# Running two gate panels ahead of the norm's root in a hybrid attention trunk

## The reference

```
h = h + mlp_sq_relu(rmsnorm(h, norm_mlp[i]), w_up[i], w_down[i])
gate = jax.nn.sigmoid(rmsnorm(h, norm_ple[i]) @ w_ple_gate[i])
h = h + gate * (p[i] @ w_ple_proj[i])
```

## Time and profile before

| | us |
|---|---|
| median of three runs | 2636.97 |
| lowest, highest | 2633.31, 2637.98 |
| profiled execution | 2633.67 |
| its span, from first to last instruction | 2632.1 |
| PE busy | 2530.4 (96%) |
| DVE busy | 1895.3 (72%) |
| ACT busy | 1144.4 (43%) |
| POOL busy | 792.5 (30%) |

### The profile page before, as it was taken

One profiled execution on the slowest core, in us unless ns is written; L12 is line 12 of the kernel. 1 busy time (PEld: TensorE's weight loads), 2 busy tenths in 40 slices (PEclk: granted clock), 3 DMA queues, 4 the chain that ended last, 5 costly groups with the idle time before them and its releaser, 6 DMA issues. The chain is left out here.

```text
span 2632.1 us, 32491 instructions
## 1 busy us (share of the span) xinstructions
PE 2530.4 (96%) x11896; PEld 2080.5 (79%) x11896; DVE 1895.3 (72%) x2562; ACT 1144.4 (43%) x1862; POOL 792.5 (30%) x586
## 2 busy tenths in 40 slices
PE   7999999899999999999999999999999998999998
PEld 6878888687888778887778888878788886888777
DVE  7677655657666789998765667566766668999876
ACT  6555433534444444444442324254444444444353
POOL 2000000023332456666420000002323336666642
PEclk9999999999999999999999999999999999999999
DMA  3000000122323432332221011112233233323112
GB/s 131 31 27 25 29 28 25 46 83 87 118 101 118 134 113 100 115 110 68 77 96 41 25 33 32 32 41 88 92 105 119 101 130 111 128 97 120 65 56 81
DMA packets 78641, 207.64 MB, mean 79 GB/s; under 512 B 8673, under 2 KB 10737, under 8 KB 78497
## 3 DMA queue, kind: packets, MB, share of 16 engines
q1 hardware_dynamic: 75552, 195.85, 21.9%
q0 software_dynamic: 2224, 7.54, 0.8%
q10 hardware_dynamic: 720, 2.36, 0.2%
HBM read 163.25 MB, written 42.47 MB: 78 GB/s over the span
## 5 line engine op out<-in xcount | busy, mean ns | idle before, releaser
L738 PE MATMUL gemm_ps<-a_hi,whi 128*128 128x512 f32 x1024 | 424.8, 415 | 19.2 <-DVE a_lo L1917 10.7
L740 PE MATMUL gemm_ps<-a_hi,wlo 128*128 128x512 f32 x1024 | 403.3, 394 | 0.0
L739 PE MATMUL gemm_ps<-a_lo,whi 128*128 128x512 f32 x1024 | 402.2, 393 | 0.0
L738 PEld LDWEIGHTS gemm_ps<-a_hi,whi 128*128 128x128 f32 x1024 | 194.4, 190 | 59.9 <-issue 20.2
L740 PEld LDWEIGHTS gemm_ps<-a_hi,wlo 128*128 128x128 f32 x1024 | 193.7, 189 | 43.0
L1245 POOL TENSOR_TENSOR hid_raw<-hid_raw 128x512 f32<-128x512 f32 x120 | 197.3, 1653 | 97.3 <-DVE a_blocks L2393 34.6
L739 PEld LDWEIGHTS gemm_ps<-a_lo,whi 128*128 128x128 f32 x1024 | 194.7, 190 | 32.8 <-issue 1.4
L2306 DVE TENSOR_TENSOR wlo<-wraw,whi 128x512 fp32r<-128x512 f32 (+1 forms) x204 | 181.0, 888 | 32.5 <-ACT whi L1601 31.9
L2306 DVE TENSOR_TENSOR wlo<-wraw_a,whi 128x512 fp32r<-128x512 f32 (+1 forms) x204 | 180.0, 883 | 33.8 <-ACT whi L1601 32.8
L1601 ACT ACTIVATE whi<-wraw_a 128x512 fp32r<-128x512 f32 (+1 forms) x204 | 122.6, 602 | 174.7 <-PE s_ps L740 134.1
L738 PE MATMUL s_ps<-b_blocks_hi,whi 128*128 128x512 f32 x448 | 178.9, 399 | 13.2 <-DVE wlo L2306 9.2
(11 more groups left out here) (390 smaller groups left out, 6376.4 us busy)
## 6 DMA issues: line engine op xcount, KB each, us to landing
wraw<-panels SPq DMA_DIRECT2D x90, 512.0 KB, 3.5
wraw<-folds SPq DMA_DIRECT2D x60, 512.0 KB, 4.3
wraw_a<-folds SPq DMA_DIRECT2D x60, 512.0 KB, 4.2
hid_raw<-hidden SPq DMA_DIRECT2D x120, 256.0 KB, 3.7
hidden<-sumsq SPq DMA_DIRECT2D x64, 256.0 KB, 3.9
hidden<-zs SPq DMA_DIRECT2D x32, 256.0 KB, 2.1
hidden<-zt SPq DMA_DIRECT2D x32, 256.0 KB, 2.0
h<-x_t SPq DMA_DIRECT2D x11, 512.0 KB, 5.3
```

Source lines behind the costliest of these rows:

```text
L738: nc.tensor.matmul(out, hi_w, hi_x, start=start, stop=False, skip_group_check=True)
L739: nc.tensor.matmul(out, hi_w, lo_x, start=False, stop=False, skip_group_check=True)
L740: return nc.tensor.matmul(out, lo_w, hi_x, start=False, stop=stop, skip_group_check=True)
```

## The change

- **PE.** Gate panel 1 is numbered before projection panel 3 and runs before the norm sums. The weight stream is put in the same order.
- **Raw units.** DVE copies the four units of gate panels 0 and 1 unscaled to SBUF (`keep_raw`, into `gate_raw`, two tiles of a_hi that lie free) and multiplies them with rstd once the root is there (`scale_raw`). ACT's sigmoid of these waits on the new semaphore `raw_scaled`.
- **ACT.** All high parts of tiles 2 to 7 come before the first square.
- **p.** The high and low part of p's first half move from block 4 to block 3 of the last turn, the low part of the first projection panel from block 4 to block 5. POOL's `tail_adds(2)` waits for that low part of p.
- **Last pair.** The four additions in SBUF leave `down_out` and come after the low part of the second projection panel (`last_adds`). Two of them change places, and the counts of `next_hi` with them.
- **DVE.** The order of copies and splits behind it is changed.

```diff
--- before.py
+++ after.py
@@ -182,7 +182,7 @@
...
     s["tail"] = s["wo"] + KT
-    s["ple"] = [s["tail"] + j for j in (0, 1, 2, 4)]
+    s["ple"] = [s["tail"] + j for j in (0, 1, 2, 5)]
     s["gate"] = s["tail"] + 3
@@ -328,6 +328,8 @@
...
+
+        gate_raw = m["p_skip"][:, 3:5].rearrange("p o (h n) -> p o h n", h=2)
         hid_raw, a_blocks = m["hid_raw"], m["a_blocks"]
@@ -442,6 +444,7 @@
...
         p_hi_ready, p_lo_ready = sem("p_hi_ready"), sem("p_lo_ready")
+        raw_scaled = sem("raw_scaled")
         sig_ready, h_ready, o_gated = sem("sig_ready"), sem("h_ready"), sem("o_gated")
@@ -1035,6 +1038,7 @@
...
                                 unit(Idx(st["gate"]), half, b_hi, b_lo, Idx(st["x_ple"]), places=places)
+                        panel(Idx(st["gate"] + 1), b_hi, b_lo)
                         norm_sums(st["norm"] + 2, to_ps)
@@ -1052,7 +1056,6 @@
...
                         last.then_inc(unit_ready, 1)
-                panel(Idx(st["tail"] + 5), b_hi, b_lo)
                 stage(Idx(st["tail"] + 6), KT - 2 - (LATE if layer else 0), b_hi, b_lo)
@@ -1306,7 +1309,7 @@
...
                 last_sums()
-                gp.wait_ge(blk_lo_ready, BLOCKS * turn_of(layer, TURNS))
+                gp.wait_ge(p_lo_ready, 2 * layer + 1)
                 tail_adds(2)
@@ -1669,7 +1672,7 @@
...
                     else:
-                        act.wait_ge(tail_last, 4 * layer + {(0, 1): 3, (1, 0): 4, (1, 1): 2}[o % 2, half])
+                        act.wait_ge(tail_last, 4 * layer + {(0, 1): 2, (1, 0): 3, (1, 1): 4}[o % 2, half])
                     A(b_hi[:, o, half_cols(half)], piece(o, half), ACT.Copy,
@@ -1735,27 +1738,35 @@
...
                             w_hi(Idx(st["tail"]))
+                        if n == LAST and j == 3:
                             act.wait_ge(p_loaded, 16 * (layer + 1))
...
                 A(p_hi[1], p_raw[:, :, half_cols(1)], ACT.Copy).then_inc(p_hi_ready, 1)
-                for o in range(6):
+                for o in range(2, 4):
                     for half in range(2):
-                        next_hi(o + 2, half)
-                        tail_square(o, half)
-                    if o in (1, 3):
-                        w_hi(Idx(st["tail"] + 2 + o // 2))
-                w_hi(Idx(st["tail"] + 4))
-                for o in (6, 7):
+                        next_hi(o, half)
+                w_hi(Idx(st["tail"] + 2))
+                for o in range(4, KT):
+                    for half in range(2):
+                        next_hi(o, half)
+                w_hi(Idx(st["tail"] + 3))
+                for o in range(KT):
                     for half in range(2):
                         tail_square(o, half)
+                    if o == 2:
+                        w_hi(Idx(st["tail"] + 4))
                 w_hi(Idx(st["tail"] + 5))
+                w_hi(Idx(st["tail"] + 6))
                 norm_root_of(st["norm"] + 2, to_ps)
                 def sigmoid(p, o, half):
-                    act.wait_ge(unit_free, p.times(2).at(half + 1))
+                    if p is None:
+                        act.wait_ge(raw_scaled, 4 * layer + o.times(2).at(half + 1))
+                    else:
+                        act.wait_ge(unit_free, p.times(2).at(half + 1))
                     act.wait_ge(sq_added, (o.times(2) + (16 * (st["norm"] + 3) + half)).at(-1))
@@ -1763,21 +1774,21 @@
...
-                def gate(o, weights=True):
+                def gate(o, weights=True, raw=False):
                     p = o + (st["tail"] + 4)
                     for half in range(2):
-                        sigmoid(p, o, half)
+                        sigmoid(None if raw else p, o, half)
                         finish_gated(o, half)
...
                 for half in range(2):
-                    sigmoid(Idx(st["gate"]), Idx(0), half)
-                w_hi(Idx(st["tail"] + 6))
+                    sigmoid(None, Idx(0), half)
+                w_hi(Idx(st["tail"] + 7))
                 for half in range(2):
                     finish_gated(Idx(0), half)
+                gate(Idx(1), False, True)
                 if layer == 0:
-                    gate(Idx(1))
                     with act.Fori(1, KT // 2 - 1) as i:
@@ -1786,10 +1797,9 @@
...
                 else:
-                    for o in range(1, KT - LATE):
-                        gate(Idx(o), o == 1)
-                        if o > 1:
-                            late_w_hi(o - 2)
+                    for o in range(2, KT - LATE):
+                        gate(Idx(o), False)
+                        late_w_hi(o - 2)
@@ -2359,9 +2369,6 @@
...
                         V.tensor_tensor(p7, b["E"], p7, ALU.add).then_inc(fold_read, 1)
-                        if n == LAST:
-                            dve.wait_ge(fold_read, read + 5)
-                            V.tensor_tensor(p7, p7, u2, ALU.add).then_inc(tail_last, 1)
                     if j == 3:
@@ -2371,15 +2378,17 @@
...
                         V.tensor_tensor(out, b["A" if j == 2 else "E" if j == 6 else "D"], out, ALU.add).then_inc(fold_read, 1)
-                    if n == LAST and j in (5, 6):
-                        if j == 5:
-                            dve.wait_ge(tail_last, 4 * layer + 1)
-                            V.tensor_tensor(piece(2 * q + 1, 1), piece(2 * q + 1, 1), p7, ALU.add).then_inc(tail_last, 1)
-                            dve.wait_ge(fold_read, read + 6)
-                            V.tensor_tensor(piece(2 * q, 1), piece(2 * q, 1), u2, ALU.add).then_inc(tail_last, 1)
-                        else:
-                            dve.wait_ge(fold_read, read + 7)
-                            V.tensor_tensor(piece(2 * q + 1, 0), piece(2 * q + 1, 0), p7, ALU.add).then_inc(tail_last, 1)
+
+                def last_adds():
+
+                    q, read = PAIRS - 1, reads(layer, LAST)
+                    u2, p7 = SUM_U2[q], SUM_P7[q]
+                    dve.wait_ge(fold_read, read + 7)
+                    V.tensor_tensor(p7, p7, u2, ALU.add).then_inc(tail_last, 1)
+                    V.tensor_tensor(piece(2 * q, 1), piece(2 * q, 1), u2, ALU.add).then_inc(tail_last, 1)
+                    dve.wait_ge(tail_last, 4 * layer + 1)
+                    V.tensor_tensor(piece(2 * q + 1, 0), piece(2 * q + 1, 0), p7, ALU.add).then_inc(tail_last, 1)
+                    V.tensor_tensor(piece(2 * q + 1, 1), piece(2 * q + 1, 1), p7, ALU.add).then_inc(tail_last, 1)
@@ -2462,11 +2471,13 @@
...
                             split_of(EARLY_TILES[n, j], 1)
-                        if n == LAST and j == 4:
+                        if n == LAST and j == 5:
                             w_lo(Idx(st["tail"]))
+                        if n == LAST and j == 3:
                             p_low(0)
...
                 w_lo(Idx(st["tail"] + 1))
+                last_adds()
                 n = st["norm"] + 3
@@ -2497,45 +2508,60 @@
...
+                def keep_raw(o, half):
+                    dve.wait_ge(unit_ready, 2 * (st["gate"] + o) + half + 1)
+                    V.tensor_copy(gate_raw[:, o, half], bank(half)).then_inc(unit_free, 1)
+
+                def scale_raw(o, half):
+                    V.tensor_tensor(zt[:, half], gate_raw[:, o, half], rstd[:, half_cols(half)],
+                                    ALU.mult).then_inc(raw_scaled, 1)
+
...
                 w_lo(Idx(st["tail"] + 2))
+                split_of(2, 0)
                 pp_out(1, 0)
-                split_of(2, 0)
                 split_of(2, 1)
+                split_of(3, 0)
                 pp_out(1, 1)
                 w_lo(Idx(st["tail"] + 3))
-                split_of(3, 0)
+                split_of(3, 1)
                 pp_out(2, 0)
-                split_of(3, 1)
-                split_of(4, 0)
-                split_of(4, 1)
+                for half in range(2):
+                    split_of(4, half)
                 pp_out(2, 1)
-                for o in (5, 6):
+                for o in (5, 6, 7):
                     for half in range(2):
...
                 w_lo(Idx(st["tail"] + 4))
-                for half in range(2):
-                    split_of(7, half)
-                w_lo(Idx(st["tail"] + 5))
+                for o in range(2):
+                    for half in range(2):
+                        keep_raw(o, half)
+                    w_lo(Idx(st["tail"] + 5 + o))
                 norm_scale(n - 1)
                 for half in range(2):
-                    gate_in(Idx(st["gate"]), half)
+                    scale_raw(0, half)
                 for e in range(2):
                     pp_out(3, e)
-                w_lo(Idx(st["tail"] + 6))
+                w_lo(Idx(st["tail"] + 7))
                 for half in range(2):
...
                         next_lo(Idx(0), 0)
+                for half in range(2):
+                    dve.wait_ge(h_ready, 16 * layer + half + 1)
+                    scale_raw(1, half)
+                    if half == 0:
+                        next_lo(Idx(0), 1)
```

(13 more changed lines are left out.)

## The result

The changed kernel takes 2639.41 us (median, 2636.63 to 2643.59) where the kernel before, run beside it, takes 2635.83 (2631.94 to 2639.16). The ratio is 1.0015, with 95% between 1.0009 and 1.0021: 4.0 us slower, 2.4 to 5.5 (the two medians differ by 3.6). That is small, 0.15%, but clear of no change, and of the other sign than the 2.7 us gained that I forecast. The profiled execution has a span of 2635.0 us, before 2632.1.

What follows compares the result with a forecast made beforehand. It took PE, busy 96% of the span, to bound the kernel. Gains of 1.3 us in layer 0 and 1.4 in layer 1 summed to 2.7, giving 2634.3 us on the median's scale, range 2625 to 2641.5.

Steps and rivals of the forecast that it cites:

- the term for the wait behind the root: New PE waiting for DVE's reading of panel 2's bank after the root: 2.0 us in layer 0, 0.5 in layer 1.
- The gap itself: PE's stop before gate panel 3, where DVE reads panel 2's bank late: 2.0 us in layer 0, 0.5 in layer 1.
- the 13.0 us: Behind the root, DVE does tile 0 as before until 13.0 us behind the sums; gate panel 1's work follows.
- Ahead of the root: Stretch up to gate panel 2, claimed to start 3.3 us earlier in layer 0 and 1.9 in layer 1.
- the gap before the fold's last block product: PE's 2.75 us wait for the fold's last product, claimed to vanish with the early low part of p.
- the gap at the second projection panel: New PE wait of 1.7 us for the first copy, behind the last pair's additions moved later.
- panel 0: Gate panel 0: PE gaps of 1.35 us at its start, 2.9 for split (5,0), 1.3 and 0.3 for tile 7.
- the last: PE's wait before gate panel 1 for the weights' low part and the first raw copy: 1.8 us.
- Less contention: Rival: POOL slows DVE's splits less ahead of gate panel 1; 2623 us at half contention, 2619 at none; 16 in 100.
- The clock falls in the new gaps: Rival: falls in gate panels 1 and 3, 2.3 us each; 2638.9 us with one per layer, 2643.5 with two; 12 in 100.
- It does nothing: Rival: the wait after the root, longer by the sigmoid's place behind the square, takes back 3.3 us; 2637 us; 12 in 100.
- The rule weighed: DVE splits beside POOL: exclusion for whole instructions would give about 1.96 us; the prediction took the trace's 1.75.

Runs made afterwards that it cites:

- whi_early: Changed kernel with ACT making the next weights' high part before finishing the gate's second half; 0.9999 of the kernel before.
- before_whi_early: Kernel before, with ACT making the next weights' high part before it finishes the gate's second half; 0.9989 of the kernel before, 2.9 us faster.
- in_place: Changed kernel, scaling raw panel 1 in its own buffer and reading panel 2's first half before finishing panel 1; 1.0014 of the kernel before.
- no_raw: Kernel before with every part of the change but the raw units, gate panel 1 staying behind the sums; 1.0021 of the kernel before, 5.5 us slower.
- raw_only: Changed kernel with only PE's order and the raw units left of the change; 1.0041 of the kernel before, 10.8 us slower.
- both_late: Changed kernel with the edits of in_place and whi_early, POOL's squares starting only when tile 4 is split; 0.9963 of the kernel before, 0.9965 in its repeat.
- both: Changed kernel with the edits of in_place and whi_early together; 0.9984 of the kernel before.
- short_sums: Changed kernel with POOL copying one column in place of fourteen of the sixteen additions of squares in each layer; 0.9978 of the kernel before.

## Why the prediction was wrong

**The step that failed** is the term for the wait behind the root, 2.0 and 0.5 us, and in it the last sentence on the scaling: "PE's next panels take 10.9 us each against DVE's 7 to 8, so this is paid once." The 7 to 8 us are DVE's busy time. Its period is 11.32 us in layer 0's loop, because each turn passes several times between DVE and ACT, and that is longer than PE's 10.9. A late start was therefore not caught up there, but grew. The term of 2.0 us in layer 0 measured 7.25: 2.88 for the gap, then 1.8 for the start of panel 4 (12.67 us behind panel 3), 1.3 for three panels at 11.32, 1.0 more for the last norm sum, and 0.3 in pauses of 0.15 us and less. The term of 0.5 in layer 1 measured 2.68: 1.39, then 1.0 more in front of the late panels, and small ones. whi_early and before_whi_early show how much of it is the chain: with the wait for ACT out of it DVE is back to waiting for PE, and the cost is 4.8 and 1.6 us. The rest is the gap and, in layer 0, the fall of the clock behind it. The waits of DVE in the trace of before, 16.3 us in seven for the high part of the weights, had it written down, and I had looked only at PE's waits.

**The gap itself was undersized**, 2.88 for 2.0 and 1.39 for 0.5. In part that is my sum: the terms listed behind the 13.0 us add up to 6.95, which ends 19.95 us behind the sums and not 19.3, and makes the gap 2.6. In part it is contention. I priced the multiplications like those from PSUM, 0.68 us. With the raw copy as source both inputs are in SBUF, and beside POOL's copies of squares (1291.02 and 1292.35) the first took 1.10 us (1291.58), the low part behind it 1.09. in_place shows that this part alone is not what decides.

**Ahead of the root the forecast held in its sum, in part by luck.** I had 3.3 us in layer 0 and 1.9 in layer 1 for panel 2, 5.2; the mean over four kernels with this code against before's is some 3 a layer. DVE was faster than I saw, which alone made it 5.7 in the one layer 0 without a fall of the clock, and falls that the forecast didn't count took 1.1 us (second projection panel) and 1.6 (gate panel 1) back in others. Single terms: the gap before the fold's last block product is gone; the gap at the second projection panel is 2.3 for 1.7 (the first of the last additions took 1.78 us beside POOL, for 1.1); panel 0 had no gap where I saw 1.35, because DVE's work up to tile 4 was faster, and 0.76 and 1.02 for 2.9 and 1.3, because a split beside POOL takes 1.53 us and not 1.73; the last, 1.94 for 1.8, is right. The sums came at 1280.4 for 1282.7 by the clock of before. What I had not asked is what each half brings: no_raw and raw_only show that neither gains alone ahead of the root over both layers.

**The rivals.** *Less contention* came half: panel 1 began 2.4 us earlier than forecast (1269.4 by the clock of before for 1271.8). *The clock falls in the new gaps* did happen: in gate panel 3 as it said, at the second projection panel of layer 1, and in gate panel 1, its other place, in five of the six stretches of the three kernels with the same code. With one fall a layer it gave a loss of 1.9 us, nearest of all to the 4.0 measured. But the falls are not the main cause: behind the root the changed kernel lost 7.25 us in layer 0, where its fall cost nothing, as said below, and 2.68 in layer 1 without one. Windows of the changed kernel (us; busy and count of PE, PEld, DVE, ACT, POOL; granted clock; DMA share; GB/s):

```profile
1299.69:1304.69 5.00, 5.00 (x15) 3.97 (x16) 3.81 (x5) 2.22 (x5) 2.06 (x2) 0.66 0.26 105
2505.00:2510.00 5.00, 5.00 (x15) 3.98 (x16) 4.30 (x5) 3.99 (x7) 0.00 (x0) 0.66 0.17 18
```

15 products in 5 us for 22 at full clock is 1.6 us, not 2.3, and the first of the two cost nothing: panel 4 had to wait for DVE's reading at 1311.62 anyway. With the chain shortened the same fall shows, since nothing covers it (behind panel 2 both_late took 76.01 us with one, and 74.48 in its repeat without). *It does nothing*, "by the sigmoid's place behind the square", was nearest in mechanism: the new wait is longer than worked out and takes the gain back. A place in ACT's queue behind a square has a part in it, but that of the next weights and not of the sigmoid, and more than the gain is taken back.

**The rule weighed.** A split beside POOL takes 1.53 us (six in 9.20) in the changed kernel, POOL's additions 1.58 (fourteen in 22.16); before they took 1.75 and 1.70. The Trainium skill, page "SBUF — State Buffer", section "Who interferes with whom", would have a split wait for the whole addition, some 1.96 us by my estimate from the durations alone; the trace doesn't bear that out. Whether they exclude each other for a shorter part of their durations no run shows. In the kind of instruction the trace agrees with it: a multiplication with both inputs in SBUF is slowed beside POOL's copy (1.10 us at 1291.58) and one that reads PSUM is not (before, 0.68 us at 1288.17, with POOL's copy from 1287.61 to 1288.73), which I left unused where the change moved the source.

**What stays open:** why before_whi_early gained 2.9 us in the medians where its rows behind the root show 2.0, why the turn is longer in the loop, and what decides whether the clock falls, since the falls come and go between executions of the same code. The gap of 2.1 us that both and both_late keep in front of panel 3's second half was left as it is.

## What to carry to other kernels

An engine that is busy for 8 of 11 us is not therefore fast: take its period, from one start of an instruction to the next start of the same one, and ask for the waits of the engine that feeds the bottleneck and not only for those of the bottleneck. Work moved ahead of a barrier adds to what is released behind it at once; where the chain behind has no slack per turn, a late start is paid to the end, and removing one gap may only move it. And try the parts of a change alone, and a repair on the kernel before as well: here two halves that each lose (10.8 and 5.5 us) lose less together (4.0), and with the chain behind them repaired and POOL's start moved the whole gains 9.7, of which the shorter chain by itself gave the old kernel 2.9.

## What the runs showed of the hardware

A DVE split that takes its inputs from SBUF and POOL's additions slow each other: to 1.53 and 1.58 us in the changed kernel, to 1.75 and 1.70 in the one before, where alone they take 0.68 and 1.29. A pair thus costs 0.2 to 0.4 us less than one after the other. Moving a multiplication's input from PSUM to SBUF has a price beside POOL: 1.10 us for 0.68.

On TensorE's clock: a wait of 2.87 or 2.88 us in front of gate panel 3 was followed by products at 0.43 us instead of 0.23, the 1.2 GHz level, in each of the four layers 0 that had it (the changed kernel, whi_early, raw_only, short_sums), and then by 2.4 GHz again. Waits of 2.3 and 1.95 us were followed by it in some executions of the same code and not in others. After 6.06 us the four sums took 3.50 us for 1.88.

A turn of the same instructions between DVE and ACT took 11.32 us in the loop and 10.54 behind it.
